# Strassen's scheme for the channel mixer of a hybrid decoder step

## The chip, the cores and the metric

The kernel runs on one core of one Trainium2 chip. The metric is the device time of one execution in microseconds (us). The engines are TensorE (PE; its weight loads are PEld), VectorE (DVE), ScalarE (ACT), GpSimd (POOL) and SyncE (SP), which here only issues DMAs.

## The reference

One layer of a decoder trunk is computed for 1024 prompt rows and 8 sample rows (1032 rows in all, width 1024). Three token mixers run side by side and are joined by an output projection; then comes the channel mixer, on which the change works:

```python
x = x + mix @ w_out                            # 1024 x 1024
hid = relu(rmsnorm(x, norm2_g) @ w_up)         # w_up 1024 x 4096
x = x + (hid * hid) @ w_down                   # w_down 4096 x 1024
```

All of it is float32, and the projections are computed to more than one fp32r product's precision: each operand is split in a high part H (a copy to fp32r) and a low part L (the rest), and a product is three matmuls, H·H + H·L + L·H.

## The kernel before

Activations are kept transposed: 128 features on the partitions, the 1032 rows along the free axis, cut in three thirds of 344 columns (`TC`). `split_product` issues the three matmuls of each 128-deep step, at lines 59, 60 and 61.

`mix_and_mixer` is the last stage. The output projection works through 24 units (`UNITS`: a third of the columns and a block of 128 outputs) of 24 matmuls; w_out's block is loaded anew for each unit, `high_out` (ScalarE, L3184) and `low_out` (VectorE, L3330) split it, `add_out` (L3337) adds the product to x. GpSimd splits the attention heads (L3058), VectorE builds and splits the other mixers' columns (L3312 to L3325). The squares of x are summed, spread by a matmul with ones, and give 1/rms after `root` and `inverse`.

The channel mixer takes the 32 hidden blocks of 128 in 16 groups of two (`FG`, `NFG`). For a group, `up` makes 6 products of 24 matmuls (8 steps deep) and `down` makes 24 products of 6 matmuls, one for each output block and third. The order on PE is up(g+1), down(g). On the other engines: `relu` (VectorE, L3372) applies relu and 1/rms to an up product, `hidden` (ScalarE, L3236 and L3238) squares it and makes its H, `low_hidden` (VectorE, L3377) its L; `high_up`/`low_up` and `high_down`/`low_down` split 1 MB of w_up and 1 MB of w_down; `add_unit` (VectorE, L3383) adds each down product onto x in SBUF. SP loads the two weight blocks when their buffer is free. x is kept in SBUF throughout. At the end 72 transposes (`turn_out`, L3164), copies and stores put out the result, most of them between the last group's products.

All order is written out by hand: each engine executes its own list, and semaphores tie the lists together.

## Time and profile before

| | before |
|---|---|
| device time, median of 3 runs | 1832.87 us (1830.13 to 1837.3) |
| span of the profiled execution | 1838.3 us |
| PE busy | 1750.0 us, 95% |
| VectorE busy | 1050.8 us, 57% |
| ScalarE busy | 634.1 us, 34% |
| GpSimd busy | 170.1 us, 9% |
| mean granted TensorE clock | 0.973 |
| DMA | 177.18 MB, mean 96 GB/s |

The profiled execution's span is 5.4 us above the median of the runs. A busy row of PE says that matmuls were in its pipeline, not that it was full; how close they follow one another is read from their starts.

### The profile page before, as it was taken

The numbers are of one execution on the slowest core, as the hardware profiler recorded it, in microseconds if no ns is written. First come the engines' busy times: TensorE is split into PE (matmuls) and PEld (weight loads), VectorE is DVE, ScalarE is ACT, GpSimd is POOL, SyncE is SP. The second block draws the span as 40 slices with busy tenths as digits, with TensorE's granted clock in tenths as the row PEclk, the third lists the DMA queues.
The fourth block names the chain that finished last, engine by engine and source line by source line (L and its number), as shares of the span: only waits on it lengthen the run. The fifth ranks groups of instructions, "written<-read, shape, count | busy, mean of one in ns | idle before, by whom it ended". The sixth has DMA issues, their size and how long they took to land. (4 is left out here: it accounts for less than half of the span.)

```text
span 1838.3 us, 32447 instructions
## 1 busy us (share of the span) xinstructions
PE 1750.0 (95%) x12947; PEld 1617.8 (88%) x12947; DVE 1050.8 (57%) x1867; ACT 634.1 (34%) x1144; POOL 170.1 (9%) x203
## 2 busy tenths in 40 slices
PE   6999999989999979999967999999999999999998
PEld 6999999978888858877735899999999999999998
DVE  6363584248877756666776675444444444444445
ACT  7523332137655544444443353111111111111111
POOL 1000000012222242222112000000000000000000
PEclk9989999979999989999977999999999999999999
DMA  7741265360000147764974651111111111111102
GB/s 186 120 98 35 58 161 150 115 173 24 14 2 1 47 146 236 235 215 149 271 187 136 182 155 47 46 46 46 46 46 46 46 46 46 46 46 46 46 24 93
DMA packets 183907, 177.18 MB, mean 96 GB/s; under 512 B 51501, under 2 KB 163205, under 8 KB 181173
## 3 DMA queue, kind: packets, MB, share of 16 engines
q1 hardware_dynamic: 175716, 132.66, 25.6%
q0 software_dynamic: 2304, 33.56, 4.8%
q10 hardware_dynamic: 5776, 9.44, 1.8%
q8 instruction: 76, 1.25, 0.3%
q14 instruction: 35, 0.28, 0.0%
HBM read 139.60 MB, written 40.23 MB: 98 GB/s over the span
## 5 line engine op out<-in xcount | busy, mean ns | idle before, releaser
L59 PE MATMUL pm<-hH,wuH 128*128 128x344 f32 x768 | 246.3, 321 | 0.0
L61 PE MATMUL pm<-hH,wuL 128*128 128x344 f32 x768 | 245.0, 319 | 0.0
L60 PE MATMUL pm<-hL,wuH 128*128 128x344 f32 x768 | 245.0, 319 | 0.0
L59 PE MATMUL pm<-hidH,weights 128*128 128x344 f32 x720 | 230.7, 320 | 0.0
L60 PE MATMUL pm<-hidL,weights 128*128 128x344 f32 x720 | 230.3, 320 | 0.0
L61 PE MATMUL pm<-hidH,weights 128*128 128x344 f32 x720 | 230.0, 319 | 0.0
L59 PE MATMUL pz<-hH,winH 128*128 128x344 f32 x600 | 200.0, 333 | 1.6 <-DVE hL L845 1.6
L60 PE MATMUL pz<-hL,winH 128*128 128x344 f32 x600 | 193.8, 323 | 0.0
L61 PE MATMUL pz<-hH,winL 128*128 128x344 f32 x600 | 193.7, 323 | 0.0
L3372 DVE SCALAR_TENSOR_TENSOR act<-pm,onat 128x344 f32<-128x344 f32 x96 | 49.3, 516 | 239.8 <-PE pm L61 239.3
L3383 DVE TENSOR_TENSOR onat<-pm,onat 128x344 f32<-128x344 f32 x256 | 129.0, 514 | 68.9 <-PE pm L61 68.9
L59 PEld LDWEIGHTS pm<-hH,wuH 128*128 128x128 f32 x768 | 144.4, 188 | 0.3
L61 PEld LDWEIGHTS pm<-hH,wuL 128*128 128x128 f32 x768 | 144.4, 188 | 0.0
L60 PEld LDWEIGHTS pm<-hL,wuH 128*128 128x128 f32 x768 | 144.0, 187 | 0.2
L60 PEld LDWEIGHTS pm<-hidL,weights 128*128 128x128 f32 x720 | 135.6, 188 | 0.0
L61 PEld LDWEIGHTS pm<-hidH,weights 128*128 128x128 f32 x720 | 135.5, 188 | 0.0
L59 PEld LDWEIGHTS pm<-hidH,weights 128*128 128x128 f32 x720 | 135.2, 188 | 0.0
L3236 ACT ACTIVATE act<-act 128x1032 f32<-128x1032 f32 x32 | 34.1, 1067 | 272.7 <-DVE act L3372 272.7
L3227 ACT ACTIVATE weights<-hs 128x2048 fp32r<-128x2048 f32 x15 | 28.7, 1914 | 266.2 <-PE pm L61 266.2
L59 PEld LDWEIGHTS pz<-hH,winH 128*128 128x128 f32 x600 | 114.9, 191 | 4.5 <-issue 3.0
L60 PEld LDWEIGHTS pz<-hL,winH 128*128 128x128 f32 x600 | 114.8, 191 | 0.9
L61 PEld LDWEIGHTS pz<-hH,winL 128*128 128x128 f32 x600 | 114.7, 191 | 0.0
(621 smaller groups left out, 3493.3 us busy)
## 6 DMA issues: line engine op xcount, KB each, us to landing
uact<-in_w_up_dram SPq DMA_DIRECT2D x15, 1024.0 KB, 6.9
hs<-in_w_down_dram SPq DMA_DIRECT2D x15, 1024.0 KB
raw<-in_w_in_dram SPq DMA_DIRECT2D x24, 512.0 KB, 3.8
hold<-vS_scratch SPq DMA_DIRECT2D x4, 2048.0 KB, 10.9
wo<-in_w_out_dram SPq DMA_DIRECT2D x12, 512.0 KB
act<-in_w_out_dram SPq DMA_DIRECT2D x12, 512.0 KB, 5.0
zT_scratch<-zb ACTq DMA_DIRECT2D x8, 516.0 KB, 2.6
hold<-in_x_prompt_dram SPq DMA_DIRECT2D x8, 512.0 KB, 4.2
```

The costliest lines, as they stand in the source:

```text
L59: nc.tensor.matmul(out, wH, mH, start=start and k == 0, stop=False)
L60: nc.tensor.matmul(out, wH, mL, start=False, stop=False)
L61: last = nc.tensor.matmul(out, wL, mH, start=False, stop=stop and k == n - 1)
L3227: nc.scalar.activation(wdH[:, :, :], wd[:, :, :], ACT.Copy).then_inc(wdH_ready, 1)
L3236: nc.scalar.activation(act2[:, f, :], act2[:, f, :], ACT.Square)
L3372: nc.vector.scalar_tensor_tensor(out=act2[:, f, cols[third]], in0=ps[third][:, 0:TC], scalar=0.0, in1=rn[:, cols[third]], op0=ALU.max, op1 ...
L3383: nc.vector.tensor_tensor(y, ps[4 + n % 4][:, 0:TC], y, ALU.add).then_inc(added, 1)
```

## The change

Channel mixer up and down are each done by one level of Strassen's scheme in Winograd's form: a product of two 2 x 2 block matrices by seven block products and sums of blocks before and behind them.

Up: two hidden blocks (a pair, `p`, 16 pairs), the two halves of the 1024 inputs, and the rows cut in four quarters of 258 columns (`CQ`; `c` counts two halves of the rows, each with two quarters). Down: the two hidden blocks and two output blocks make the 2 x 2 blocks; four pairs of outputs are kept as `acc` (`NM` = 4), and the hidden pairs are taken two at a time, in 8 groups (`NGRP`); a block `M` is one group and one pair of outputs, 32 in all.

The two phases no longer alternate. First all 16 pairs go up. What is left of a pair are seven hidden operands, H and L, 516 columns each: they go through a ring of four SBUF buffers to DRAM (`hidD`, `store_hid`). Then all 32 blocks go down, and `load_hid` brings the operands back, seven loads per group, into the buffer that held the inputs' operands. x goes to DRAM (`xS`, `keep_x`) and comes back as the accumulators' start (`load_acc`).

Engines: GpSimd makes the four sums of the weights (`add_weights`), of x (`x_first` to `x_fourth`) and of the hidden blocks (`add_hidden`), and adds products in the downward phase (`accumulate`), which it gets through a staging copy on ScalarE (`stage_copy`). VectorE evicts the products with additions (`evict`, `take`) and makes all L parts. 1/rms is now applied to x (`scale_x`) ahead of the mixer. The PSUM tensors are four of two banks; three of them take the products in turn. The output projection works in 16 units of 516 columns.

```diff
+                def store_hid(p, o):
+                    n = 7 * p + o
+                    sp.wait_ge(hidL_ready, n + 1)
+                    sp.dma_start(hidD[p, :, HID_PLACE[o], :], ring[n % 4].rearrange("p s t -> p (s t)")).then_inc(hid_stored[n % 4], 16)
+
+                def load_hid(g, j):
+                    if g < 2:
+                        sp.wait_ge(prod_done, made(NPAIR - 1, j))
+                    else:
+                        sp.wait_ge(prod_done, made2(4 * (g - 2) + 3, j))
...
+                for g in range(NGRP):
+                    load_weights(NPAIR + 2 * g + 2)
+                    if g + 2 < NGRP:
+                        for j in range(7):
+                            load_hid(g + 2, j)
+                    load_weights(NPAIR + 2 * g + 3)
...
+                def add_weights(v):
+                    pool.wait_ge(w_in, 16 * (v + 1))
+                    if v:
+                        pool.wait_ge(wL_ready, 7 * (v - 1) + 5)
+                    nc.gpsimd.tensor_tensor(sum_of(v, 0), block_of(v, 1, 0), block_of(v, 1, 1), ALU.add).then_inc(s_ready, 1)
+                    nc.gpsimd.drain()
+                    nc.gpsimd.tensor_tensor(sum_of(v, 1), sum_of(v, 0), block_of(v, 0, 0), ALU.subtract).then_inc(s_ready, 1)
+                    nc.gpsimd.tensor_tensor(sum_of(v, 2), block_of(v, 0, 0), block_of(v, 1, 0), ALU.subtract).then_inc(s_ready, 1)
+                    if v:
+                        pool.wait_ge(wL_ready, 7 * v)
+                    nc.gpsimd.drain()
+                    nc.gpsimd.tensor_tensor(sum_of(v, 3), block_of(v, 0, 1), sum_of(v, 1), ALU.subtract).then_inc(s_ready, 1)
...
+                def add_hidden(p):
+                    pool.wait_ge(bA_ready, 2 * p + 1)
+                    pool.wait_ge(bD_ready, 2 * p + 2)
+                    if p:
+                        pool.wait_ge(hidL_ready, 7 * (p - 1) + 5)
+                    nc.gpsimd.tensor_tensor(T1, C12, C11, ALU.subtract).then_inc(t_ready, 1)
...
+                def accumulate(M):
+                    m = M % NM
+                    for n, j in enumerate((0, 1, 3, 4)):
+                        a = acc[m][:, 0 if n < 2 else 4, :]
+                        pool.wait_ge(evA, takenA(M, j))
...
+                for p in range(1, NPAIR):
+                    add_hidden(p - 1)
+                    add_weights(p + 1)
+                add_hidden(NPAIR - 1)
+                for u in range(NPAIR - 2):
+                    accumulate(2 * u)
+                    add_weights(NPAIR + u + 1)
+                    accumulate(2 * u + 1)
...
+                def up(p, j, chunks):
+                    for c in chunks:
+                        last = split_product(nc, bank_of(p, j)[:, c, :], [(slots[:, j, 0, k * P:(k + 1) * P], slots[:, j, 1, k * P:(k + 1) * P]) for k in range(4)],
+                                             [(ops[:, c, j, k, 0, :], ops[:, c, j, k, 1, :]) for k in range(4)])
+                    last.then_inc(prod_done, 1)
+
+                def down(b, M, j):
+                    at = lambda k: slice((2 * k + M % 2) * P, (2 * k + M % 2 + 1) * P)
+                    for c in range(2):
+                        cols = slice(c * CQ, (c + 1) * CQ)
+                        last = split_product(nc, bank_of(NPAIR + M, j)[:, c, :], [(slots[:, j, 0, at(k)], slots[:, j, 1, at(k)]) for k in range(2)],
+                                             [(ops2[:, b, j, k, 0, cols], ops2[:, b, j, k, 1, cols]) for k in range(2)])
+                    last.then_inc(prod_done, 1)
...
+                for p in range(1, NPAIR):
+                    for j in range(7):
+                        pe.wait_ge(wL_ready, 7 * p + j + 1)
+                        if j < 3:
+                            pe.wait_ge(evD, evicted(p - 1, j + 5))
+                        if j == 3:
+                            pe.wait_ge(evA, copied(p))
+                        if j >= 4:
+                            pe.wait_ge(evD, evicted(p, j - 3))
+                        up(p, j, (0, 1))
```

ScalarE's and VectorE's lists for a pair (the first part of each is for pair p and what is left of p-1; the weights are those of p+1):

```diff
+                for p in range(1, NPAIR):
+                    first_copy(p)
+                    high_w(p + 1, 0)
+                    high_hid(p - 1, 3)
+                    high_hid(p - 1, 4)
+                    high_w(p + 1, 1)
+                    high_hid(p - 1, 5)
+                    relu_square(p, C11, 2)
+                    high_w(p + 1, 2)
...
+                for p in range(1, NPAIR):
+                    finish(p - 1)
+                    low_hid(p - 1, 2)
+                    low_w(p, 6)
+                    low_w(p + 1, 0)
+                    evict(p, 1)
+                    low_hid(p - 1, 3)
+                    low_hid(p - 1, 4)
+                    low_w(p + 1, 1)
+                    evict(p, 2)
+                    low_hid(p - 1, 5)
+                    low_w(p + 1, 2)
+                    evict(p, 3)
+                    low_hid(p - 1, 6)
+                    low_w(p + 1, 3)
+                    evict(p, 4)
+                    evict(p, 5)
+                    low_hid(p, 0)
+                    low_w(p + 1, 4)
+                    evict(p, 6)
+                    relu2(C21)
+                    low_hid(p, 1)
+                    low_w(p + 1, 5)
```

In the first stage, the store of x for the 8 sample rows becomes four DMAs with pieces of two columns, since each quarter takes two of these rows.

## Rows read from the trace of the kernel before

**Rows 1.** The page: TensorE's busy time, and the clock granted in 40 slices (tenths).
```profile
PE 1750.0 (95%) x12947; PEld 1617.8 (88%) x12947; DVE 1050.8 (57%) x1867; ACT 634.1 (34%) x1144; POOL 170.1 (9%) x203
...
PEclk9989999979999989999977999999999999999999
```

**Rows 2.** Windows: stretch, its length, busy time (operations) by engine, clock, DMA share, GB/s.
```profile
991.23:1095.80 104.57, 97.98 (x596) 95.47 (x595) 71.33 (x107) 47.16 (x72) 7.46 (x6) 0.97 0.58 176
1095.80:1829.30 733.50, 732.74 (x4662) 731.61 (x4660) 360.47 (x586) 139.41 (x134) 0.00 (x0) 1.00 0.14 47
1829.30:1838.30 9.00, 3.02 (x24) 2.55 (x24) 2.57 (x4) 1.79 (x3) 0.00 (x0) 0.96 0.54 188
950.00:960.00 10.00, 6.87 (x30) 3.23 (x28) 7.92 (x15) 6.94 (x10) 0.00 (x0) 1.00 1.05 385
...
1200.00:1300.00 100.00, 100.00 (x637) 100.00 (x636) 49.92 (x82) 16.17 (x14) 0.00 (x0) 1.00 0.12 42
```

**Rows 3.** Groups of instructions: count, busy us, mean ns of one, idle before.
```profile
L59 PE MATMUL pm<-hH,wuH 128*128 128x344 f32 x768 | 246.3, 321 | 0.0
...
L3383 DVE TENSOR_TENSOR onat<-pm,onat 128x344 f32<-128x344 f32 x256 | 129.0, 514 | 68.9 <-PE pm L61 68.9
...
L3377 DVE TENSOR_TENSOR hidL<-act,hidH 128x1032 fp32r<-128x1032 f32 x32 | 39.2, 1224 | 0.0
```

**Rows 4.** Timeline of PE: start us, duration us, instructions.
```profile
523.82 0.28 PE L1401 MATMUL pS<-kHL,qS 128*128 128x256 f32 x1
523.94 0.28 PE L1402 MATMUL pS<-kLH,qS 128*128 128x256 f32 x1
524.06 0.23 PE L1404 MATMUL pS<-diag_r,ident_r 128*128 128x128 f32 x1
...
988.97 1.12 PE L3066 MATMUL pm<-ident,onat 128*128 128x128 f32 x4 [3.84 <-DVE tmpm L3314]
...
992.23 0.49 PE L59 MATMUL pm<-hH,weights 128*128 128x344 f32 x1
992.52 0.49 PE L60 MATMUL pm<-hL,weights 128*128 128x344 f32 x1
```

**Rows 5.** Timeline of VectorE in the output projection.
```profile
1002.45 1.78 DVE L3325 TENSOR_TENSOR hL<-act,hH 128x512 fp32r<-128x512 f32 x1
...
1007.19 0.69 DVE L3325 TENSOR_TENSOR hL<-act,hH 128x512 fp32r<-128x512 f32 x1
1007.80 0.51 DVE L3337 TENSOR_TENSOR x<-pm,x 128x344 f32<-128x344 f32 x1
...
1008.80 0.47 DVE L3314 SCALAR_TENSOR_TENSOR tmpm<-pm,gains,uact 128x256 f32<-128x256 f32 x1
...
1012.97 0.48 DVE L3314 SCALAR_TENSOR_TENSOR tmpm<-pm,gains,uact 128x256 f32<-128x256 f32 x1
1013.53 1.18 DVE L3319 TENSOR_TENSOR act<-tmpm,gates_mix 128x256 f32<-128x256 f32 x1
```

**Rows 6.** Timeline of GpSimd in the same stretch.
```profile
984.82 4.22 POOL L3058 TENSOR_TENSOR hL<-onat,hH 128x512 fp32r<-128x512 f32 x3 [7.66 <-ACT hH L3188]
1001.87 1.81 POOL L3058 TENSOR_TENSOR hL<-onat,hH 128x512 fp32r<-128x512 f32 x1 [12.82 <-ACT hH L3188]
...
1008.39 1.29 POOL L3058 TENSOR_TENSOR hL<-onat,hH 128x512 fp32r<-128x512 f32 x1 [3.00 <-ACT hH L3188]
1013.14 1.29 POOL L3058 TENSOR_TENSOR hL<-onat,hH 128x512 fp32r<-128x512 f32 x1 [3.46 <-ACT hH L3188]
```

**Rows 7.** DMA issues: count, KB each, us to landing.
```profile
uact<-in_w_up_dram SPq DMA_DIRECT2D x15, 1024.0 KB, 6.9
...
win_rows<-in_cache_nsa_win_dram SPq DMA_DIRECT2D x1, 4096.0 KB, 17.9
```

**Rows 8.** Groups on VectorE: a reciprocal, and an operation with a scalar.
```profile
L932 DVE RECIPROCAL hold<-hold 128x344 f32<-128x344 f32 x18 | 41.3, 2295 | 0.0
...
L3341 DVE SCALAR_TENSOR_TENSOR hL<-onat,g,hH 128x344 fp32r<-128x344 f32 x16 | 8.6, 573 | 0.0
```

More of the change, by code:

```diff
@@ new lines, in mix_and_mixer @@
+        T1x = hsf[:, D:D + 4 * CQ].rearrange("p (k t) -> p k t", k=4)
+        raw = uact[:, :, :].rearrange("p a t -> p (a t)")[:, 0:2 * D]
+        stage = [wo0[:, 0:2 * CQ], wo0[:, 2 * CQ:4 * CQ], hsf[:, 3 * 512:3 * 512 + 2 * CQ]]
+        up_raw = raw.rearrange("p (j k i n) -> p j k i n", j=2, k=4, i=2)
+        dn_raw = raw.rearrange("p (k j d i n) -> p k j d i n", k=2, j=2, d=2, i=2)
+        s1, U2, U3, C11, C12, T1, C21, C22 = (unit[n] for n in range(8))
+        ring = [late[:, (16 + 4 * n) * CQ:(20 + 4 * n) * CQ].rearrange("p (s t) -> p s t", s=2) for n in range(4)]
@@ new lines, in mix_and_mixer @@
+        hid_of = {0: C11, 1: C22, 2: C21, 3: C12, 4: T1, 5: C22, 6: C21}
+        acc = [acc0[:, :, :]] + [late[:, 10 * n * CQ:10 * (n + 1) * CQ].rearrange("p (a t) -> p a t", a=5) for n in range(NM - 1)]
+        ynat = [ynat_flat[:, 512 * n:512 * (n + 1)] for n in range(4 * NM)]
+        smp = smp_flat[:, :].rearrange("p (m i c h r) -> p m i c h r", m=NM, i=2, c=2, h=2)
+        ysn = ysn_flat[:, :].rearrange("p (m x) -> p m x", m=NM)
+        bank = [ctx.enter_context(nc.psum_tensor(f"pm{i}", [P, 1024], F32)) for i in range(4)]
@@ L3168, in _ @@
[L3168 to L3175 removed]
+                    else:
+                        pe.wait_ge(t_used, TQ)
+                    for h in range(2):
+                        last = nc.tensor.matmul(whole[3][:, h, :], ones[:, :], part(squares[c][0], h), start=True, stop=True)
@@ new lines, in _ @@
+                square(15)
+                first_copy(0, 0)
+                root(1)
+                for o in range(5):
+                    high_x(1, o)
+                first_copy(0, 1)
+                high_x(1, 5)
+                high_x(1, 6)
+                for j in range(2):
+                    high_w(1, j)
+                relu_square(0, C11, 2)
+                high_w(1, 2)
+                high_hid(0, 0)
+                high_w(1, 3)
+                relu_square(0, C22, 4)
+                high_w(1, 4)
@@ L3380, in add_unit @@
[L3380 to L3393 removed]
+                    nc.vector.tensor_tensor(mixc[:, b % 2, 2:4, 0:n], tmp[:, :, 0:n], mo[:, :, at], ALU.mult).then_inc(mixc_ready, 1)
@@ new lines, in low_hid, with evict @@
+                def low_hid(p, o):
+                    n = 7 * p + o
+                    dve.wait_ge(hidH_ready, n + 1)
+                    nc.vector.tensor_tensor(ring[n % 4][:, 1, :].bitcast(F32R), hid_of[o], ring[n % 4][:, 0, :], ALU.subtract).then_inc(hidL_ready, 1)
+                PLACE = {1: (1, s1, U2), 2: (2, s1, C11), 3: (3, U2, U3), 4: (4, U3, C22), 5: (4, U2, U2), 6: (5, U3, C21), 7: (6, U2, C12)}
+                def evict(p, e, c=None):
+                    j, other, out = PLACE[e]
+                    dve.wait_ge(prod_done, made(p, j) if c != 0 else j + 1)
+                    if e == 1:
+                        dve.wait_ge(evA, copied(p) if c != 0 else 1)
+                    if e == 2 and p:
+                        dve.wait_ge(t_ready, 4 * (p - 1) + 1)
+                    if e in (3, 4, 7):
+                        nc.vector.drain()
+                    if p:
+                        nc.vector.tensor_tensor(both(out), bank_of(p, j), both(other), ALU.add).then_inc(evD, 1)
+                    else:
+                        nc.vector.tensor_tensor(part(out, c), bank_of(0, j)[:, c, :], part(other, c), ALU.add).then_inc(evD, 1)
@@ new lines, in _ @@
+                for k in range(4, 8):
+                    scale_x(1, k)
+                for o in range(6):
+                    low_x(1, o)
+                evict(0, 1, 1)
+                low_x(1, 6)
+                evict(0, 2, 1)
+                low_w(1, 0)
+                evict(0, 3, 1)
+                low_w(1, 1)
+                evict(0, 4, 1)
+                evict(0, 5, 1)
+                low_w(1, 2)
+                low_hid(0, 0)
+                evict(0, 6, 1)
+                relu2(C21)
```

1086 lines of the change are left out of this document (686 added, 400 removed).

## The prediction

> **What bounds the kernel now.** The page comes first: TensorE's matmul row is busy for 95% of the span, and the granted clock is nine tenths or more in nearly every slice of the second half [rows 1]. The windows then cut the span where the change begins. The output projection runs from 991.2 to 1095.8 us, the channel mixer from there to 1829.3, and 9.0 us are left for the last transposes, copies and stores [rows 2]. In the mixer PE is busy 732.7 of 733.5 us at clock 1.00, while VectorE is busy for half of it, ScalarE for a fifth, GpSimd not at all, and the DMAs move 47 GB/s. A busy PE row is no proof of a full PE, since each matmul lasts 320 ns by the groups [rows 3] though they start much closer: one full-clock stretch holds 637 matmuls in 100 us, so one starts every 157 ns [rows 2]. The mixer's 4608 matmuls at 0.157 are 724 us of its 733; most of the rest are 72 transposes. So the mixer is bound by matmuls, the only thing that the change makes fewer of, and everything else there has half its time free. The question is what the new work does to the free half.
>
> The profiled span is 1838.3 us; the median of the runs is 1832.9, so I work the sum against the span and take off 5.4 us at the end. What a measurement of this kernel can tell from no change is about 0.5%, some 9 us.
>
> **TensorE.** A group of 256 columns starts every 0.12 us (523.82, 523.94, 524.06) [rows 4], 344 columns every 0.157; at half clock 344 take 0.287 (992.23 to 992.52) [rows 4]. The distance thus is columns at 2.4 GHz (107 ns and 143 ns) plus about 13 to 14 ns. 258 columns cost 0.120 us, bounds 0.118 and 0.123. The new mixer has 16 pairs x 7 products x 2 chunks x 12 = 2688 matmuls up, and 32 x 7 x 2 x 6 = 2688 down, 5376 in all: 645 us for 724. Seven eighths of the columns would be 634; the smaller pieces give 11 us back. The gain of a matmul-bound kernel is 79 us, and that is the ceiling of the change. The Trainium skill ("TensorE: Matmul & The Clock Gate", Back-to-back issue gap) gives columns over 2.4 GHz plus 2.5 ns. By it 344 columns would be 146 ns and 258 would be 110. The trace has 157 for the first, so I keep 0.120 in the sum.
>
> **Output projection.** 24 units of 24 matmuls become 16 x 48 of 258 columns: 768 x 0.12 = 92.2 us. With four groups of transposes (2), a slow clock at the start (10 matmuls, 1.4), a sum (0.9) and small waits (1.0) it is 97.5 for 104.6 us before; w_out is loaded 16 times, not 24, and 11.5 us of matmuls cover two loads where 7.5 did. Five blocks are mixed ahead of it for three, and gates_mix loads grow by a third: it starts some 1.5 us later. The three more tiny stores of x in the first stage (8 bytes a piece) stand on SP's queue ahead of small constants, and the stage's weights have a buffer's lead; I give them 0, and 7 us, about a landing, if that cover is gone.
>
> **The upward phase, one pair of hidden blocks.** PE needs 168 x 0.12 = 20.2 us. Vector has, per pair: seven lows of weights and seven of hidden blocks plus two squarings, all with two SBUF operands, 16 operations of 512 or 516 columns. A 512-column one starts 0.61 us before the next (1007.19 to 1007.80) [rows 5], together 9.8 us. Six evictions of 516 columns from PSUM: 344 take 514 ns [rows 3], 172 more columns at 0.96 GHz add 179, less 0.08 of overlap: 0.61 each, 3.7. Five drains at about 0.16 (1012.97 plus 0.40 against 1013.53) [rows 5]: 0.8. That is 14.3 of 20.2 us, and would hide.
>
> But GpSimd, idle before, gets eight two-operand sums per pair (four of weights, four of hidden). One such operation of 512 columns takes 1.29 us, and three in a row that began behind a vector operation took 4.22 [rows 6], 1.18 each. And they exclude Vector: while GpSimd ran from 1001.87 to 1003.68, the vector subtraction at 1002.45 took 1.78 us, where the same line takes 0.69 at 1007.19 [rows 5, 6]. The 256-column product at 1013.53 took 1.18, and ended just behind GpSimd's 1013.14 plus 1.29. The PSUM-fed one at 1008.80 wasn't held up (0.47), with GpSimd busy since 1008.39. So a vector operation with two SBUF operands waits for GpSimd's, and the other way round; one that reads PSUM doesn't. From these rows GpSimd holds Vector off for some 1.1 us a time. The Trainium skill ("SBUF — State Buffer", Who interferes with whom) calls it an exclusive lock, held for the whole instruction, and the trace agrees.
>
> I follow one pair by its order of instructions, time 0 being the last eviction of the pair before. Eviction, drain and squaring of C12 to 1.5; low_hid; GpSimd's T1; low_w(p, 6); C12's sum; low_w(p+1, 0); eviction 1 beside C22's sum (6.1); low_hid 3; C21's sum; low_hid 4 to 8.9. Now Vector wants low_w(p+1, 1), for which ScalarE needs the second sum of weights. GpSimd does its sums of weights behind those of the hidden blocks: it is there at 11.2, ScalarE's copy at 11.9. So Vector waits 3 us. Then low_w 1, eviction 2 (13.6), low_hid 5, a wait of 0.9 for relu, square and high_w on ScalarE, low_w 2, eviction 3 (17.0), low_hid 6, low_w 3, evictions 4 and 5 (19.6), low_hid 0, a wait of 0.7, low_w 4, eviction 6, a squaring, low_hid 1 and low_w 5, to 24. Added up: 14.3 of work, 4.8 of lock and 4.6 of waits are 23.7; I take 24.0 with the semaphores. PE needs eviction 2 for product 5 and stands there for 3.4 us; it has 3.8 to spare. Bounds: 20.2 if GpSimd's operations fall into Vector's gaps, 26 if the clock drops in PE's gaps. The weights (1 MB, 6.9 us to land [rows 7]) and 3.7 MB of stores per pair don't bind: 4.8 MB are 12.5 us at the 385 GB/s that a full queue moved [rows 2]. Pairs 1 to 15: 15 x 24 = 360 us.
>
> **Pair 0.** Its first half (seven products of 12) needs 11 us with the waits for single evictions. Meanwhile the second half of x must be normalised: root 4.5 us after the projection's end, a reciprocal of 516 columns at 2.3 us per 344 [rows 8], 3.4; eight scalings at 0.7 (573 ns for 344 columns [rows 8]); GpSimd's four sums of 1032 columns at 2.3 us; seven lows of 1032 columns at 1.22 [rows 3] and as many highs on ScalarE; again one after the other on the same lock. xL for the second half's first product is there at about 19, for the others from 28, and PE, cold at first (rows at half clock: 0.287 for 0.157), ends at 39, where 21 would do. Bounds 30 and 45.
>
> **The downward phase.** 32 x 84 x 0.12 = 322.6, 72 transposes as before, 8. Vector has six PSUM-fed additions per block and 3.5 lows, 6 us of 10.1; ScalarE four copies and 3.5 highs. GpSimd has 12 sums per two blocks, 14.2 us plus drains and lock, some 18 of 20.2: it keeps up, with 2 us to spare. The loads are the other matter: a group of four blocks (40.3 us) reads 7.4 MB of hidden sums in seven loads, and 2.1 MB of weights. At 385 GB/s that is 25 us, so the mean fits. But the seven loads are issued during 10 us, and the weights of the next but one block queue behind them: they land 15 us after their block's start and not 9.6. GpSimd's sums, ScalarE's copy behind high_w and the staging of product 4 are late, and PE stands 2.6 us; six times, 16. At the hand-over the last pair's stores, 14.8 MB of loads for two groups, 3 MB of residual and 3 MB of weights have to pass within 61 us: 25 MB at 385 GB/s are 65. By the order of SP's queue the last load of group 0 is 2.6 us late, the weights behind group 1's loads land 8 to 9 us too late, and their effect lingers for 2: 14 us, bounds 5 and 45. Sum 361.
>
> **Sum.** 991.2 + 1.5 + 97.5 + 39 + 360 + 361 + 10 (the end, 9.0 before, plus a drain more) = 1860 us for 1838.3. Less 5.4: 1855 us, 1.2% slower.
>
> **Rivals.**
> (a) The lock costs little and the upward phase goes at PE's pace, 20.2 us a pair. That is 57 us less: 1798, faster. For it: Vector has only 14.3 us of work per pair, and my order of who gets the lock first is. Against it: the rows of 1002.45 and 1013.53 [rows 5]. It decides between 22.5 and 23 us a pair; below 22.5 the kernel is faster. Chance 0.28.
> (b) The forecast: lock and waits bind, 1855, own range 1835 to 1885. Chance 0.43.
> (c) The loads bind the downward phase. The one 4 MB load took 17.9 us [rows 7], 234 GB/s; at that rate a group needs 40.4 us of transfers for its 40.3 of PE, every late load counts, and the hand-over's 25 MB need 107 us: 45 us more, 1900. Against it: 385 GB/s in a full queue [rows 2]. Chance 0.14.
> (d) PE's gap of 3.4 us in each pair lets the granted clock fall: PE had stood idle for 3.84 us before the transposes at 988.97, and the projection's first ten matmuls ran at 0.287 [rows 4], which is 1.2 GHz. Two products at half clock are 4.7 us longer, of which 2.5 aren't covered: 37 us, 1892. Chance 0.12.
> (e) Small matmuls have no 13 ns beside their columns: 0.110 us. For it: nothing in the rows but that 0.12 is read off two intervals of 256 columns. The 768 and the 2688 downward matmuls, where PE sets the pace, would be 35 us shorter: 1820. Chance 0.03.
>
> **The numbers.** Below 1823.7 lie (a), (e) and a thin lower edge of (b): faster 0.32. Within 0.5%: 0.12, from the lower part of (b). Slower: the rest of (b), (c) and (d), 0.56. The range 1790 to 1900 leaves out half of (a)'s lower side and the worst of (c) and (d).
>
> **What would show it.** Right: in the upward phase VectorE's row is near full, its SBUF-only lows of 516 columns have a mean well above 0.69 us while evictions stay at 0.69; 24 us from one pair to the next; PE waits for an eviction in mid pair. In the downward phase PE waits come in six places, behind ScalarE's staging copies and the weights' DMA. Matmuls start 0.120 us apart when nothing is late. Wrong: lows at 0.7 us and pairs at 20.2 would refute the lock's price, a DMA row above nine tenths for long the rate, and a clock below 1.00 in the upward phase would be (d).

## The result, and the profile after

| | before | after |
|---|---|---|
| device time, median of 4 runs each | 1833.7 us (1830.1 to 1837.3) | 1904.8 us (1901.2 to 1908.0) |
| span of the profiled execution | 1838.3 us | 1901.4 us |
| PE busy | 1750.0 us, 95% | 1705.2 us, 90% |
| VectorE busy | 1050.8 us | 1266.3 us |
| GpSimd busy | 170.1 us | 690.5 us |
| DMA | 177 MB | 301 MB |

The change makes the kernel 4.0% slower: the ratio is 1.040, 95% interval 1.037 to 1.043. The forecast was 1.2% slower, 1855 us, with a range up to 1900. The sign was right, the size was not, and the time lies outside the range.

The page of the changed kernel, busy time and then the 40 slices, answers to [rows 1]:

```profile
PE 1705.2 (90%) x13909; PEld 1558.3 (82%) x13909; DVE 1266.3 (67%) x1958; ACT 810.1 (43%) x1565; POOL 690.5 (36%) x568
PE   7799999989999989999769868888888879999998
PEclk9899999989999989999889979899999989999999
```

Before, TensorE's row was nines almost throughout the mixer. Now it has eights from slice 25 to 32 (the upward phase) and a seven at 33 (the hand-over). The windows of the same kernel (columns as in [rows 2]): output projection, pair 0, pairs 1 to 14, the hand-over between the phases, and the downward phase.

```profile
990.00:1100.00 110.00, 105.03 (x862) 103.80 (x861) 81.06 (x84) 41.88 (x57) 47.65 (x26) 1.00 0.47 150
1100.00:1140.00 40.00, 24.41 (x174) 23.91 (x173) 33.13 (x35) 15.65 (x23) 20.95 (x11) 0.74 0.17 50
1140.00:1480.00 340.00, 292.09 (x2229) 285.57 (x2228) 255.51 (x306) 143.07 (x254) 164.25 (x110) 0.94 0.54 191
1480.00:1560.00 80.00, 66.86 (x510) 65.07 (x508) 53.85 (x69) 30.77 (x55) 37.86 (x28) 0.94 0.93 353
1560.00:1830.00 270.00, 241.73 (x1930) 236.88 (x1931) 175.42 (x222) 101.22 (x177) 201.81 (x142) 0.97 0.56 213
```

No engine is full anywhere; the DMA engines nearly are in the hand-over (0.93) and only there. In the upward phase TensorE is busy for 86%, VectorE for 75%, and the DMA engines for 54%, so what costs is waiting, and the question is who waits for whom. Against the terms of the forecast, each stage read from the first matmul of one part to the first of the next:

| stage | forecast, us | measured, us |
|---|---|---|
| start of the output projection | 992.7 | 986.1 |
| output projection | 97.5 | 101.5 |
| pair 0 | 39 | 42.3 |
| pairs 1 to 15 | 15 x 24.0 = 360 | 15 x 25.35 = 380.3 |
| downward phase | 361 | 383.8 |
| end | 10 | 7.5 |

The sum is 41 us above the forecast's 1860, and two terms make 43 of it: the pairs, 20.3, and the downward phase, 22.8; the others nearly cancel. The remaining 9 us between 1855 and 1904.8 are the step from span to median: I took off 5.4 as before, but here the median is 3.4 above the profiled span.

**A pair.** VectorE's timeline from the end of one pair to the middle of the next (start, duration, the idle time before it in brackets), then GpSimd's, then the one row of ScalarE that explains the first gap:

```profile
1313.10 0.69 DVE L3769 TENSOR_TENSOR onat<-onat 128x516 fp32r<-128x516 f32 x1
1313.70 1.79 DVE L3764 TENSOR_TENSOR slots<-hs,slots 128x512 fp32r<-128x512 f32 x1
1319.24 0.89 DVE L3764 TENSOR_TENSOR slots<-uact,slots 128x512 fp32r<-128x512 f32 x1 [3.75 <-ACT slots L3555]
1320.05 0.68 DVE L3783 TENSOR_TENSOR onat<-pm,onat 128x516 f32<-128x516 f32 x1
1320.66 2.86 DVE L3769 TENSOR_TENSOR onat<-onat 128x516 fp32r<-128x516 f32 x2
1323.66 1.54 DVE L3764 TENSOR_TENSOR slots<-hs,slots 128x512 fp32r<-128x512 f32 x1
1325.12 0.68 DVE L3783 TENSOR_TENSOR onat<-pm,onat 128x516 f32<-128x516 f32 x1
...
1313.31 1.63 POOL L3276 TENSOR_TENSOR onat<-onat 128x516 f32<-128x516 f32 x1 [11.80 <-issue]
1315.10 1.55 POOL L3279 TENSOR_TENSOR onat<-onat 128x516 f32<-128x516 f32 x1 [0.16 <-issue]
...
1319.53 1.72 POOL L3241 TENSOR_TENSOR hs<-uact 128x512 f32<-128x512 f32 x1
1321.41 1.54 POOL L3243 TENSOR_TENSOR hs<-hs,uact 128x512 f32<-128x512 f32 x1 [0.16 <-issue]
...
1318.57 0.63 ACT L3555 ACTIVATE slots<-uact 128x512 fp32r<-128x512 f32 x1 [6.42 <-DMA uact<-in_w_up_dram]
```

The lock is there as forecast: the subtraction at 1313.70 takes 1.79 us beside GpSimd's sum, two at 1320.66 take 2.86 (1.3 when nothing is beside them), and an eviction from PSUM keeps its 0.68. What I had not put in is the 3.75 us gap. It belongs to weight block 0 of the next pair. Its transfer is issued only when the last block of the one raw buffer has been read, at the end of the pair, and ScalarE gets it 6.4 us after it became free for it. Behind it in VectorE's list stands eviction 1 (1320.05), which TensorE waits for; behind block 1 (1323.66), which waits for GpSimd's second weight sum (ready at 1322.95), stands eviction 2 (1325.12).

The first copies of the pairs are not evenly spaced. Eight of the fourteen distances are 24.7 to 25.2 us, six are 26.0 to 26.4. In each of the six, ScalarE waited 6.9 us or more for the weights, in each of the eight 6.6 or less. The pair above is a short one. In the next, a long one, the same step starts later and is stretched by the lock as well:

```profile
1344.81 1.36 DVE L3764 TENSOR_TENSOR slots<-uact,slots 128x512 fp32r<-128x512 f32 x1 [4.49 <-ACT slots L3555]
```

**The downward phase.** The first staging copies of successive blocks are 10.0 to 10.9 us apart, except for the first block (19.6), the fourth (21.5), one block in each of five groups (14.9, 15.4, 15.1, 14.6 and 16.0) and the last ones, which share TensorE with the transposes of the output. (These are distances between copies. TensorE itself began the phase at 1510.1, and the first copy at 1514.2 was some 2 us late behind ScalarE's work for the last pair.) In the third group GpSimd and ScalarE show why:

```profile
1631.37 1.27 POOL L3241 TENSOR_TENSOR hs<-uact 128x512 f32<-128x512 f32 x1 [6.47 <-DMA uact<-in_w_down_dram]
1631.33 0.63 ACT L3555 ACTIVATE slots<-uact 128x512 fp32r<-128x512 f32 x1 [3.60 <-DMA uact<-in_w_down_dram]
```

SyncE had issued seven hidden transfers from 1607.0 to 1616.0 and these weights at 1620.2; they landed at 1631.3, 11.1 us later. The block that was running had begun at about 1615.4.

### The profile page after: what moved, and what is told of

Same layout as the page of the kernel before. It is cut to its first block and busy times, and to the rows that moved or that the text cites. A ratio compares the mean times of both kernels' runs of the same rounds, so it can differ in the third digit from the quotient of the medians.

```text
span 1901.4 us, 35561 instructions
## 1 busy us (share of the span) xinstructions
PE 1705.2 (90%) x13909; PEld 1558.3 (82%) x13909; DVE 1266.3 (67%) x1958; ACT 810.1 (43%) x1565; POOL 690.5 (36%) x568
## 5 line engine op out<-in xcount | busy, mean ns | idle before, releaser
L59 PE MATMUL pm<-ops,slots 128*128 128x258 f32 x1792 | 527.3, 294 | 109.9 <-DVE onat L3783 52.5
L60 PE MATMUL pm<-ops,slots 128*128 128x258 f32 x1792 | 519.6, 290 | 0.0
L61 PE MATMUL pm<-ops,slots 128*128 128x258 f32 x1792 | 517.1, 289 | 0.0
L59 PEld LDWEIGHTS pm<-ops,slots 128*128 128x128 f32 x1792 | 350.5, 196 | 124.4 <-DVE slots L3764 57.0
L61 PEld LDWEIGHTS pm<-ops,slots 128*128 128x128 f32 x1792 | 353.2, 197 | 0.0
L60 PEld LDWEIGHTS pm<-ops,slots 128*128 128x128 f32 x1792 | 352.8, 197 | 0.0
L3764 DVE TENSOR_TENSOR slots<-uact,slots 128x512 fp32r<-128x512 f32 x128 | 116.0, 906 | 103.4 <-ACT slots L3555 103.4
L3917 DVE TENSOR_TENSOR onat<-pm,onat 128x516 f32<-128x516 f32 x144 | 99.8, 693 | 83.2 <-ACT wo L3592 44.6
L3555 ACT ACTIVATE slots<-uact 128x512 fp32r<-128x512 f32 x128 | 79.5, 621 | 132.6 <-DMA uact<-in_w_up_dram 94.1
L3764 DVE TENSOR_TENSOR slots<-hs,slots 128x512 fp32r<-128x512 f32 x93 | 113.7, 1223 | 19.7 <-ACT slots L3555 18.6
L865 DVE TENSOR_TENSOR zb<-pz,rstd 128x344 f32<-128x344 f32 x69 | 35.4, 514 | 125.0 <-PE pz L61 124.5
L3769 DVE TENSOR_TENSOR onat<-onat 128x516 fp32r<-128x516 f32 x112 | 105.8, 955 | 2.9 <-ACT onat L3569 2.9
L1548 DVE TENSOR_REDUCE nm<-pS 128x1 f32<-128x384 f32 (+7 forms) x112 | 86.4, 782 | 25.5 <-PE pS L1409 21.8
L3592 ACT ACTIVATE wo<-pm 128x516 f32<-128x516 f32 x86 | 51.6, 600 | 109.6 <-PE pm L61 95.5
## 6 DMA issues: line engine op xcount, KB each, us to landing
hold<-vS_scratch SPq DMA_DIRECT2D x4, 2048.0 KB, 11.1
```

What stands on the lines that cost most here:

```text
L59: nc.tensor.matmul(out, wH, mH, start=start and k == 0, stop=False)
L60: nc.tensor.matmul(out, wH, mL, start=False, stop=False)
L61: last = nc.tensor.matmul(out, wL, mH, start=False, stop=stop and k == n - 1)
L865: nc.vector.tensor_tensor(dst, Z[n % 3][:, 0:TC], rstd[:, cols[third]], ALU.mult).then_inc(z_copied, 1)
L1548: nc.vector.reduce_max(nm[:, s % 4, 0:n], bank[:, 0:n * TILES(i, branch) * P].rearrange("p (h c) -> p h c", h=n), AX.X, negate=True).then_ ...
L3555: nc.scalar.activation(shaped(slots[:, j, 0, :], v), weight_of(v, j), ACT.Copy).then_inc(wH_ready, 1)
```

## The experiments

Two disputes. In the upward phase: does VectorE's capacity with the lock set the pair, or one of the waits, or the order of its list? In the downward phase: do the weights come late because of the transfers ahead of them? All twelve kernels start from the changed one. "Pair" is the mean distance of the 15 first copies of pairs 1 to 15; "down" runs from the first staging copy of the downward phase to the last matmul of line 59. The ratios are each to runs of the kernel before made beside them, whose median was 1833.7 us for the changed kernel, 1836.2 for e1 to e4, 1831.9 for e5 to e8, 1831.6 for e9 and e10 and 1832.6 for e11 and e12; across these groups the ratios compare better than the times.

| run | time, us | ratio to before | 95% interval | pair, us | down, us |
|---|---|---|---|---|---|
| changed kernel | 1904.8 | 1.040 | 1.037 to 1.043 | 25.40 | 379.4 |
| e1 | 1905.1 | 1.037 | 1.033 to 1.041 | 24.76 | 380.2 |
| e2 | 1866.2 | 1.017 | 1.014 to 1.021 | 22.09 | 379.9 |
| e3 | 1839.7 | 1.002 | 1.000 to 1.004 | 20.17 | 379.4 |
| e4 | 1875.0 | 1.022 | 1.018 to 1.026 | 25.14 | 341.8 |
| e5 | 1865.8 | 1.020 | 1.018 to 1.022 | 21.96 | 380.4 |
| e6 | 1875.0 | 1.026 | 1.023 to 1.030 | 25.19 | 345.9 |
| e7 | 1829.4 | 0.998 | 0.996 to 1.001 | 21.96 | 346.3 |
| e8 | 1834.9 | 1.003 | 1.001 to 1.005 | 21.96 | 351.1 |
| e9 | 1833.2 | 1.001 | 0.999 to 1.003 | 22.08 | 346.7 |
| e10 | 1917.7 | 1.047 | 1.043 to 1.050 | 25.87 | 378.1 |
| e11 | 1815.3 | 0.991 | 0.989 to 0.992 | 21.06 | 344.0 |
| e12 | 1805.6 | 0.985 | 0.983 to 0.988 | 20.30 | 342.0 |

Three kernels with the same upward phase (changed, e4, e6) have pairs of 25.40, 25.14 and 25.19, 25.2 in the mean, so a pair is known to some 0.3 us.

### e1: small transfers of the up weights

```diff
-                    sp.dma_start(raw.rearrange("p (k n) -> p k n", k=KD), w_up[:, :, v * 2 * P:(v + 1) * 2 * P]).then_inc(w_in, 16)
+                    n = 2 * P if v < 2 else 8
+                    sp.dma_start(raw.rearrange("p (k n) -> p k n", k=KD)[:, :, 0:n], w_up[:, :, v * 2 * P:v * 2 * P + n]).then_inc(w_in, 16)
```

> Leaves out: for pairs 2 to 15 only 8 of each 256 columns of the up weights are transferred, so old weights are used; every engine does the same instructions. Theory L (the wait for the next pair's weights, whose transfer can only be issued when Vector has read the last block of the one raw buffer, lies on the Vector chain): ScalarE's idle time on the weights' transfer falls from 94 us to under 40, Vector's 3.7 us idle before the first weight difference of each pair goes, the pair falls from 25.4 to 22.5 us or less, the time by 35 to 50 us. Theory X (Vector's own work plus the lock with GpSimd set the pair, the wait only takes up slack that another wait would take): pair 24.5 us or more, time down by 15 us at most.

ScalarE's wait for the transfer fell to a third, as theory L says, but the time did not move, as theory X says, and the pair fell by 0.4 to 0.6 us. The waits between 1140 and 1480 (who waited for whom: us in total, times, longest), of the changed kernel and then of this one:

```profile
ACT slots L3555 <- DMA uact<-in_w_up_dram: 94.1, 14, 7.5
DVE slots L3764 <- ACT slots L3555: 78.4, 41, 4.8
...
PE pm L59 <- DVE onat L3783: 47.9, 35, 3.3
ACT slots L3555 <- POOL hs L3243: 32.5, 14, 2.9
```

```profile
ACT slots L3556 <- POOL hs L3244: 77.5, 14, 7.2
DVE slots L3765 <- ACT slots L3556: 64.5, 41, 3.3
...
ACT slots L3556 <- DMA uact<-in_w_up_dram: 31.0, 13, 3.0
```

63 us of waiting for the DMA went, and 45 us came back one step later, as waiting for GpSimd's second weight sum. GpSimd does its four hidden sums first (from 1299.94), then the weights' first and second sum, which is done at 1309.84, whether the weights have long been there or not. What the edit gained is about what the long pairs had lost: six times 1.3 us over fourteen distances is 0.5 to 0.6 us a pair (an estimate).

### e2: small sums on GpSimd; e3: both

```diff
+                    few = lambda a: a[:, :, 0:8] if 2 <= v < NPAIR else a
-                    nc.gpsimd.tensor_tensor(sum_of(v, 0), block_of(v, 1, 0), block_of(v, 1, 1), ALU.add).then_inc(s_ready, 1)
+                    nc.gpsimd.tensor_tensor(few(sum_of(v, 0)), few(block_of(v, 1, 0)), few(block_of(v, 1, 1)), ALU.add).then_inc(s_ready, 1)
...
+                    few = lambda a: a[:, 0:8] if p else a
-                    nc.gpsimd.tensor_tensor(T1, C12, C11, ALU.subtract).then_inc(t_ready, 1)
+                    nc.gpsimd.tensor_tensor(few(T1), few(C12), few(C11), ALU.subtract).then_inc(t_ready, 1)
```

> Leaves out: GpSimd's sums of weights (weight sets 2 to 15) and of hidden blocks (pairs 1 to 15) work on 8 columns of each block in place of 512 or 516, with all waits kept; the sums are incomplete. Theory X (lock): Vector's stretched operations fall back to 0.69 us each, 4.2 us a pair, and the pair goes from 25.4 to about 21 us, the time down by 55 to 70 us. Theory L: the lock's 4 us are gone from Vector's busy time, but the weights still land 6.9 us after the last block was read, the pair stays at 23.5 us or more, time down by 30 us at most.

> Both edits together (leaves out what both leave out). Both theories: nothing but TensorE's own products is left, pair at 20.2 us, time down by about 75 us to 1830. If the pair stays above 21.5 us, there is a third cost in the pair (ScalarE's list or TensorE's clock).

The pair in e2 is 22.09 us, between the two forecasts (21 and 23.5 or more). The lock is gone, as VectorE's groups of e2 between 1180 and 1430 show; in the changed kernel the same groups have means of 961, 796 and 1362 ns:

```profile
L3785 DVE TENSOR_TENSOR onat<-pm,onat 128x516 f32<-128x516 f32 x81 | 54.9, 691 | 3.6 <-issue 0.4
L3771 DVE TENSOR_TENSOR onat<-onat 128x516 fp32r<-128x516 f32 x79 | 53.4, 687 | 0.0
L3766 DVE TENSOR_TENSOR slots<-uact,slots 128x512 fp32r<-128x512 f32 x46 | 32.3, 703 | 68.4 <-ACT slots L3557 68.4
L3766 DVE TENSOR_TENSOR slots<-hs,slots 128x512 fp32r<-128x512 f32 x34 | 23.4, 689 | 8.7 <-ACT slots L3557 8.7
```

This edit takes away two things at once, the lock and the lateness of GpSimd's sums, and can't tell them apart. The time fell by 39 us, by the ratios 42, where theory X wanted 55 to 70. The third row keeps 68 us of waiting for the weights. That wait is worth 0.4 to 0.6 us a pair while GpSimd's sums are there (e1) and 1.9 us once they are not (e2 to e3). Against 25.2, one alone is worth 0.5, the other alone 3.2, both 5.1: each hides behind the other. In e3 TensorE is full, 250.00 of 250 us with 2093 matmuls, one every 0.119 us:

```profile
1180.00:1430.00 250.00, 250.00 (x2093) 250.00 (x2093) 185.73 (x290) 136.68 (x241) 32.79 (x96) 1.00 0.52 193
```

### e4: a quarter of the hidden transfers

```diff
+                    n = TT if g == 0 else TT // 4
-                    sp.dma_start(ops2[:, g % 2, j, :, :, :].bitcast(F32).rearrange("p k s t -> p k (s t)"),
-                                 hidD[2 * g:2 * g + 2, :, j, :].rearrange("k p x -> p k x")).then_inc(hid_in[g % 2][j], 16)
+                    sp.dma_start(ops2[:, g % 2, j, :, :, :].bitcast(F32).rearrange("p k s t -> p k (s t)")[:, :, 0:n],
+                                 hidD[2 * g:2 * g + 2, :, j, 0:n].rearrange("k p x -> p k x")).then_inc(hid_in[g % 2][j], 16)
```

> Leaves out: of the hidden operands of groups 1 to 7 only a quarter of each row is transferred back, so old operands are used. Theory Q (a weight transfer queued behind or beside seven hidden transfers of 1 MB comes late): the 5.3 us lost in every group of four blocks of the downward phase and most of the 21 us of the hand-over go, time down by 35 to 45 us. Rival R (the accumulations of GpSimd and Vector or the bank order set these stalls): time down by 10 us at most.

Theory Q. The downward phase is 37.6 us shorter; the time fell by 30 us, by the ratios 33, a little less than the 35 to 45 expected. All blocks of the five groups are 10.0 to 10.8 us apart, and the fourth block takes 11.5 us in place of 21.5. The first block keeps its 19.3 us. The edit can't speak for it, since group 0's loads stay whole (so they do in e6). The changed kernel's trace shows two causes there. ScalarE's copies for the last pair wait 4.3 us for GpSimd's sums and 2.3 and 5.3 us for stores, and the staging copies stand behind them in its list, for which TensorE waits 1.98 us. And TensorE's longest wait, 4.66 us, ends when the last hidden load of group 0 lands: issued at 1514.72, it took 13.7 us, with the DMA engines full at 384 GB/s.

```profile
1520.28 0.36 PE L59 MATMUL pm<-ops,slots 128*128 128x258 f32 x1 [1.98 <-ACT wo L3592]
...
1528.47 0.55 PE L59 MATMUL pm<-ops,slots 128*128 128x258 f32 x1 [4.66 <-issue]
```

### e5: a later place for the weight steps

```diff
                     low_w(p, 6)
-                    low_w(p + 1, 0)
                     evict(p, 1)
                     low_hid(p - 1, 3)
                     low_hid(p - 1, 4)
-                    low_w(p + 1, 1)
+                    low_w(p + 1, 0)
                     evict(p, 2)
                     low_hid(p - 1, 5)
-                    low_w(p + 1, 2)
+                    low_w(p + 1, 1)
                     evict(p, 3)
+                    low_w(p + 1, 2)
                     low_hid(p - 1, 6)
-                    low_w(p + 1, 3)
                     evict(p, 4)
                     evict(p, 5)
+                    low_w(p + 1, 3)
                     low_hid(p, 0)
-                    low_w(p + 1, 4)
                     evict(p, 6)
                     relu2(C21)
+                    low_w(p + 1, 4)
```

ScalarE's list follows: its copy of block 0 goes behind two hidden blocks, that of block 1 behind `relu_square(p, C11, 2)`.

> Same work; in the lists of Vector and ScalarE the next pair's weight blocks are taken one to three steps later in a pair, so that evictions 1 and 2 no longer stand behind weight block 0 (which waits for its transfer) and block 1 (which waits for GpSimd's second weight sum). Theory O (the order of Vector's list: the evictions that TensorE waits for stand behind steps that have most of a pair to spare): the pair falls from 25.4 to 20.5 to 22.5 us, time down by 45 to 70 us. Theory K (Vector's capacity: 14.9 us of work and 4.2 us of lock and the rest of its waits move to the new places): pair 24 us or more, time down by 20 us at most.

Theory O. The same work, bytes and lock, and the pair falls from 25.4 to 21.96 us. This is as much as e2 gains by taking GpSimd's work away. The time fell by 39 us, less than 45 to 70 and less than 14 x 3.4 = 48 in the pairs; the profiled execution began its output projection 6.6 us later than that of the changed kernel (more on this below).

### e6: the hidden transfers spread over SyncE's list

```diff
-                for j in range(2, 7):
-                    load_hid(1, j)
+                load_hid(1, 2)
+                load_hid(1, 3)
                 for g in range(NGRP):
                     load_weights(NPAIR + 2 * g + 2)
+                    if g + 1 < NGRP:
+                        for j in range(4, 7):
+                            load_hid(g + 1, j)
+                    load_weights(NPAIR + 2 * g + 3)
                     if g + 2 < NGRP:
-                        for j in range(7):
+                        for j in range(4):
                             load_hid(g + 2, j)
-                    load_weights(NPAIR + 2 * g + 3)
```

> Same work and same bytes; SyncE's list only: of the seven 1 MB hidden transfers of a group, four are issued behind one weight transfer and three behind the next, and in the hand-over the third weight set goes ahead of the last three hidden transfers of group 1. Theory Q (weights late behind the seven transfers in a row): the 5.3 us lost per group and part of the 21 us of the hand-over go, time down by 25 to 38 us. Rival V (the volume, not the order, costs: TensorE's and the other engines' accesses or the transfers themselves are slowed by any transfer beside them): time down by 10 us at most.

Theory Q again, and without leaving anything out: down 345.9 for 379.4. The five long blocks are gone (10.0 to 11.2 us), the fourth takes 14.3. Here are the windows from 1560 to 1830 of e6 and then of e4. At more than twice the transfers of e4, TensorE is as busy, so it is the order and not the volume:

```profile
1560.00:1830.00 270.00, 264.81 (x2188) 262.65 (x2187) 196.38 (x250) 114.03 (x197) 226.38 (x159) 1.00 0.59 229
```

```profile
1560.00:1830.00 270.00, 268.52 (x2226) 267.05 (x2226) 196.88 (x253) 114.98 (x198) 227.03 (x159) 1.00 0.32 96
```

### e7: both orders; e8: half transfers of the weights too

In e8 each weight transfer is two of 512 KB with a semaphore each, the first issued when blocks 0 to 3 have been read:

```diff
-                        sp.wait_ge(wL_ready, 7 * (v - 1) + 6)
+                        sp.wait_ge(wL_ready, 7 * (v - 1) + (4 if r == 0 and v != NPAIR else 6))
```

> Both orders. Theories O and Q: the gains add, 1904 less 75 to 105 us, 1800 to 1830 us, the kernel before's 1834 or below it. Theories K and V: above 1875 us.

> As both orders, and each weight transfer is split into two of 512 KB, the first issued when blocks 0 to 3 have been read. If the landing of the weights still ends a wait in the pair, another 5 to 20 us go; if the reordering has taken it off the chain, no change beyond 5 us.

The gains add (75 us, for 39 and 30 alone): 1829.4, level with the kernel before (0.998, interval 0.996 to 1.001). Splitting the transfers brings nothing to the pair, 21.96 in both, so the reordering had taken the landing off the chain. In the downward phase e8 is 5 us longer: nearly every second block takes 10.8 us there, where most of e7's take 10.0 to 10.1. Why wasn't followed up.

### e9: evictions 2 and 3 earlier

In e7 a timeline of TensorE shows just two waits in a pair, for eviction 2 and eviction 3:

```profile
1310.95 0.36 PE L59 MATMUL pm<-ops,slots 128*128 128x258 f32 x1 [0.90 <-DVE onat L3786]
1314.52 0.36 PE L59 MATMUL pm<-ops,slots 128*128 128x258 f32 x1 [0.45 <-DVE onat L3786]
```

```diff
                     evict(p, 1)
+                    evict(p, 2)
                     low_hid(p - 1, 3)
                     low_hid(p - 1, 4)
                     low_w(p + 1, 0)
-                    evict(p, 2)
+                    evict(p, 3)
                     low_hid(p - 1, 5)
                     low_w(p + 1, 1)
-                    evict(p, 3)
                     low_w(p + 1, 2)
```

> As e7, and in Vector's list evictions 2 and 3 each stand one step group earlier: eviction 2 ahead of the low parts of hidden blocks 3 and 4 and of weight block 0. In e7 TensorE waits 0.9 us for eviction 2 and 0.45 us for eviction 3 in each pair and nothing else. Theory O (order): both waits go, the pair falls from 21.96 to 20.2 to 20.8 us, time down by 15 to 25 us against e7, about 1808, below the kernel before by over 1%. Theory K (Vector's capacity: 19 us of work and lock in a pair leave no room): the waits move to another eviction, pair 21.5 us or more, time within 7 us of e7.

A miss for theory O, and what theory K had forecast: the pair is 22.08, the time within 4 us of e7. Both waits went and one of 1.67 us came, for eviction 5:

```profile
1324.31 0.36 PE L59 MATMUL pm<-ops,slots 128*128 128x258 f32 x1 [1.67 <-DVE onat L3786]
```

VectorE's busy time rose with it, from 220.4 to 236.6 of 250 us: the same work, which now meets GpSimd's operations more often.

### e10: filler matmuls in TensorE's two waits

```diff
+                        if j in (4, 5):
+                            for _ in range(8):
+                                nc.tensor.matmul(spare[0][:, 0:P], ones[:, :], ident[:, :], start=True, stop=True)
```

> The changed kernel with 16 matmuls more in each pair (8 of 128x128 FP32 before the wait for eviction 1 and 8 before that for eviction 2), into a PSUM tile that nothing reads; the rest unchanged. The theory of the clock (the gaps of 2 us at these two waits let the clock fall to 0.5 for a few us, which lengthens the pair): granted clock 1.0 in the pairs, pair down by 1 us or more, time down by 15 us or more. Theory O (Vector's list sets the pair, TensorE has slack there): clock up, pair within 0.4 us of 25.4, time within 8 us.

In the changed kernel, behind a wait of 1.94 us that ended at 1276.31, matmuls start 0.21 us apart from 1277.5 to 1280.6 and 0.12 before, which is the clock at 1.2 GHz; such stretches bring the windows to 0.91 to 1.00. With the fillers the window from 1150 to 1480 is at 1.00, and the pair is 25.87, not shorter. The pair is 0.47 us longer, and the time 13 us, a little more than theory O allows: the second group of fillers (1311.28, 1.95 us long) outlasted its wait, and product 5 started right behind it (1313.37), with no engine named as waited for. Since the fillers had a price of their own, e10 alone doesn't exclude that the clock had one too. The changed kernel's own trace does. Here are two pairs in a row, the first with a slow stretch of 15 matmuls and the second without; product 5 starts at 1403.02, 1427.83 and 1452.63, so both take 24.8 us:

```profile
1403.00:1427.80 24.80, 22.14 (x168) 21.78 (x169) 18.92 (x24) 10.79 (x20) 12.21 (x9) 0.93 0.55 193
1427.80:1452.60 24.80, 20.89 (x168) 20.35 (x168) 18.81 (x24) 10.67 (x20) 12.20 (x9) 1.00 0.54 193
```

The theory of the clock falls.

### e11: evictions 4 and 5 earlier; e12: two ReLU-squares on ScalarE

e11 moves `evict(p, 4)` and `evict(p, 5)` ahead of `low_w(p + 1, 2)` and `low_hid(p - 1, 6)`, with a drain before eviction 6. e12 takes `relu2` from VectorE:

```diff
                     evict(p, 6)
-                    relu2(C21)
...
                     high_w(p + 1, 5)
+                    relu_square(p, C21, 6)
                     high_hid(p, 2)
                     high_w(p + 1, 6)
+                    relu_square(p, C12, 7)
```

> As e9, and evictions 4 and 5 stand ahead of weight block 2 and hidden block 6 in Vector's list (the one wait of TensorE left in e9's pairs, 1.67 us, was for eviction 5). Theory K (Vector has 22.0 us of work, lock and issue in a pair, with 0.5 us idle): the wait moves on, pair 21.7 to 22.3 us, time within 6 us of e9. Theory O (order): pair 20.2 to 20.8, time down by 18 us or more against e9.

> As e11, and the ReLU and square of hidden blocks C21 and C12, 0.70 us each on Vector with a drain before each, go to ScalarE, which does them as two operations each like the other two blocks. Theory K: Vector's pair falls by 1.5 us, the pair from 22.0 to 20.3 to 20.8 us, time down by 18 to 25 us against e9 and e7, to 1805 to 1815 us, about 1% below the kernel before. Rival S (GpSimd's chain of sums, which then starts 0.6 us later, or the rest of the lock sets the pair): pair 21.5 us or more, time within 8 us of e9.

e11 lies between the two theories: 21.06, and 18 us less than e9. So e9's 22.0 us on VectorE were no fixed load; by the order alone its busy time fell from 236.6 to 233.9 in 250 us while pairs became shorter, 20.9 to 19.7 us a pair. e12 is at 20.30, nearly TensorE's own pace (20.17 in e3), and 1805.6 us: 1.5% below the kernel before (0.983 to 0.988). Its window between 1180 and 1430, and two groups of VectorE in it:

```profile
1180.00:1430.00 250.00, 249.80 (x2069) 248.36 (x2069) 214.91 (x262) 163.85 (x285) 145.33 (x98) 1.00 0.68 239
```

```profile
L3772 DVE TENSOR_TENSOR onat<-onat 128x516 fp32r<-128x516 f32 x87 | 83.9, 975 | 7.5 <-ACT onat L3568 7.5
L3767 DVE TENSOR_TENSOR slots<-uact,slots 128x512 fp32r<-128x512 f32 x50 | 46.8, 937 | 0.9 <-ACT slots L3556 0.9
```

This last step is not one of order: it takes 1.4 us of work a pair off VectorE, as theory K had forecast, and brings 0.76 us. The lock is still there (975 and 937 ns for 0.69 us of work), and costs next to nothing now.

## Why the prediction was wrong

By its own steps:

- **The ceiling, the price of a matmul: right.** 0.119 us measured against 0.120. The Trainium skill ("TensorE: Matmul & The Clock Gate", Back-to-back issue gap) gives 0.110 by its formula for an isolated matmul (an estimate from its columns over 2.4 GHz plus 2.5 ns); e3's full window shows that this stream doesn't reach it. Rival (e) falls. Rival (a), the pair at 20.2 us, needed a reordered list; as built the kernel was never near it.
- **Work and lock on VectorE: right in the sum, with some luck.** I had 14.3 + 4.8 = 19.1 us a pair; 188.05 us busy of 250 at 25.4 us a pair are 19.1. But without the lock e3 has 185.73 us of 250 at 20.17, which is 15.0 us of work and leaves 4.1 for the lock: two small errors that cancel. Evictions from PSUM stayed at 0.69 us, and in e2 all of the stretching went with GpSimd's work. The Trainium skill ("SBUF — State Buffer", Who interferes with whom) says that a VectorE instruction with two inputs in SBUF contends with a GpSimd instruction that reads SBUF, and one with at most one such input does not. The trace agrees: 961 ns in the mean against 687 without GpSimd's work, and 689 against 691 for the evictions. My sentence that VectorE's row would be near full contradicted my own sum: 19.1 of 25.4 is three quarters.
- **The waits in a pair: the step that failed first.** I had 4.6 us and took 24.0 with the semaphores; it is 25.35, times 15 is 20 us more. In the pair shown above VectorE waits 3.75, 0.84 and 0.72 us, 5.3 in all, and in a long pair more. I followed one pair from time 0 with low_w(p+1, 0) ready when VectorE came to it, and wrote that the weights "don't bind". I had checked only their rate. The transfer can't be issued before the last block of the pair before has been read, so ScalarE gets it 6.9 us later (1311.63 to 1318.57) and not in time. Counted from the start of the last eviction (1311.70), the operation behind eviction 1 starts at 9.0 us where I had 6.1. Much of that was hidden, because I had a wait for GpSimd's second weight sum just behind it, and that one was right: the sum was ready at 11.25 us, forecast 11.2. So in a short pair eviction 2 is only 0.4 us late (14.0 for 13.6) and the end 0.8 (24.8 for 24.0). In the six long pairs the weights come later still and cost 1.3 us more, which is the 0.4 to 0.6 us a pair that e1 gives back. The other 0.8 us are partly the lock (block 1's subtraction took 1.54 us) and else not settled.
- **What to call the cause.** I named the lock. e2 puts 3.2 us a pair on GpSimd's operations (lock and late sums together), e5 takes 3.3 us away with all of them in place. The lock and both late inputs cost because evictions stood behind steps that had most of a pair to spare. e5 and e11 show that by order alone, down to 21.06 us. The last 0.8 us took work off VectorE (e12). And not every move helps: e9 undid two waits and made a third.
- **The downward phase: the mechanism was right, the size was not.** "2.6 us; six times, 16" measured about 5.1 us in five groups, 25 us. The landing itself was forecast well: I had it 15 us after the block's start, and it came at about 16 (1615.4 to 1631.3). What I priced too low was its effect: every step behind it (GpSimd's sums, ScalarE's copies, staging) started late in a row, and TensorE lost 5.1 us where I had 2.6. The hand-over's 14 us were 21, and some 2 more before the first copy: 9.6 in the first block, which e4 and e6 don't touch, and 11.4 in the fourth, of which e4 removes 10.0 and e6 7.2. I had the last load of group 0 come 2.6 us late; TensorE waited 4.66 for it. e6 gives 33.5 us of the phase back.
- **Rival (c)**, the rate of 234 GB/s: refuted. In the hand-over the DMAs moved 353 GB/s in the window, and e6 is fast at the same volume. The volume does bind for a while in the hand-over, at 384 GB/s from 1512 to 1550. **Rival (d)**, the clock: it does fall in TensorE's gaps, to 0.94 over the phase, but this has no price while VectorE's list sets the pair (24.8 us with a slow stretch and without). Both rivals, 1900 and 1892, were near the measured time, for reasons that weren't there.
- **Small terms.** The output projection took 4.0 us more and pair 0 3.3, which wasn't followed up, the end 2.5 less. The 1.18 us that I took for a GpSimd sum don't follow from the row that I cited (4.22 for three is 1.4 each); in the changed kernel they take 1.3 to 1.7. The start, 6.6 early in this profile, is no part of the change's price: in the thirteen profiles of kernels with the same code up to there, the projection began between 986.1 and 1002.6 us, 996 in the mean. I had moved it by 1.5 and given it no range. It may also be why stage gains and times differ by up to 10 us in the table.
- **The range.** It took its upper end from one rival at a time. Two terms of like size missed on the same side, each by 20 to 23 us within its own bounds (26 a pair; 45 at the hand-over; the six stalls of 16 us in all had none), and a range for the sum has to allow for that.

## What to carry to other kernels

When an engine works off a list in order, ask of every step in it what stands behind it and who waits for that: a step with a whole stage to spare, put ahead of one that TensorE needs, turns each late input into TensorE's idle time, and moving it takes nothing away from the work. Read the new trace after each move, since the wait can go to the next eviction (e9). Taking away one of two late inputs showed next to nothing here (0.5 us) though both together were worth 5.1, so a wait is priced only with its neighbour gone too. And a single buffer that is refilled only when its last piece has been read needs its landing time in the sum, not only its rate; large transfers in a row are best spread between the urgent ones.

## What the runs showed of the hardware

- The start of a stage 990 us into the program varied by 16 us between profiled executions with the same instructions up to there, while the four times of the changed kernel lie within 7 us.
- Between two orders of the same instructions VectorE's busy time per pair went from 19.1 to 20.9 us (changed kernel, e9) and back to 19.7 (e11). The operations with two SBUF inputs were stretched more or less beside GpSimd's (L parts of the weights read from `uact`: 796, 1244 and 956 ns), and the evictions stayed at 0.69 us.
- FP32R matmuls of 258 columns with a weight load each start every 0.119 us at full clock, and every 0.21 us at 1.2 GHz.
- A 1 MB transfer that was issued behind seven others of 1 MB in the last 13 us landed 11.1 us after its issue. In e6 each such transfer has the hidden loads, three or four at a time, behind it, and about 18 us pass before the next is issued: GpSimd's waits for these transfers from 1600 to 1700 us were 4.3 us, not 15.3.
- The two kinds of pair in the changed kernel differ by 1.3 us, as ScalarE's wait for the weights was up to 6.6 us or 6.9 and more.
